# The rows of x loaded ahead of the modulation weights, and their preparation moved into the first unit's slots

## The chip, the cores and the metric

One core of a Trainium2 chip runs the whole program. A core has five engines with an instruction queue each: TensorE (PE, matrix multiplies), VectorE (DVE), ScalarE (ACT), GpSimd (POOL) and SyncE (SP), which here issues every transfer. Engines meet only through semaphores. The metric is the device time of one execution in microseconds (us); lower is better. TensorE's clock has two levels, 2.4 and 1.2 GHz; the profile gives the granted share.

## What is computed

A trunk of two layers over x (1024 rows of 1024, float32). Only the beginning of layer 0 is touched:

```python
shift, scale, gate = ada_modulation(c, a_ada_w[l], a_ada_b[l], 3)   # silu(c) @ w + b
u = rms_norm(h, a_norm_g[l]) * (1 + scale) + shift                  # h = x in layer 0
q, k, v, z = jnp.split(u @ a_w_in[l], 4, axis=-1)
q = rms_norm(q.reshape(bsz, seq, 2 * A_HEADS, A_HEAD_DIM), a_q_norm_g[l])
k = rms_norm(k.reshape(bsz, seq, 2 * A_HEADS, A_HEAD_DIM), a_k_norm_g[l])
...
o = diff_causal_attention(q, k, v, lam, slopes_a)
o = rms_norm(o, a_subln_g[l]) * (1.0 - lambda_init)
o = o.reshape(bsz, seq, A_INNER) * jax.nn.silu(z)
h = h + gate * (o @ a_w_out[l])
```

Then a shared key and value are made from h, and layer 1 attends to them in a window of 128 and adds its own output in the same way.

## The kernel before

**Numbers.** Projections are float32 products in three passes: each factor is split into a rounded part (u_hi, w_hi) and its remainder (u_lo, w_lo), and PE adds u_hi w_hi, u_hi w_lo and u_lo w_hi (L469 to L471). ACT writes the rounded parts, DVE or POOL the remainders.

**The prologue**, in this order:
- SP loads parameters, then the eight 1 MB chunks of the modulation weights (ada_w, 128 x 2048 each) into two buffers in turn, e0 and stage. DVE multiplies each by its column of silu(c) and adds it into adabuf (L1268, L1271), and a buffer is loaded again when DVE is done with it. Then SP loads four chunks of w_a into raw.
- PE adds adabuf up over the partitions with 16 matmuls of one column (L669), DVE makes mod (shift, scale) and smod from it (L1275, L1278).
- Then the row tiles. A row tile is 128 rows of x. For each of eight: load into half of e0, squares summed (ACT, L896), variance (DVE, L1286), seed of the root (ACT, L908 and L910), three Newton steps (DVE, L949 to L954), normalise (DVE, L1296), eight transposes of 128 x 128 into ps_t or ps_s (PE, L680), modulate columns 0 to 3 (DVE, L959) and 4 to 7 (ACT, L903) into e1, u_hi (ACT, L914), u_lo (DVE, L1299). Two tiles are under way at a time. PE projects tiles 0 and 1 of the first unit between the last of these. Of w_a's eight chunks ACT (L693) makes w_hi[0] and POOL (L394) w_lo[0] between the tiles.

**The units.** Layer 0's attention has eight units, one per head, each of eight slots, one per row tile. It is a pipeline written out by hand: in slot i of unit u PE does, in this order, the scores of tile i-3 (L488); the projection of tile i-1, chunks 0 to 2; the second part of the scores, if tile i-3 has one (from tile 4 on); the product with v of tile i-4 (L522); chunk 3; the transposes of qn of tile i-2 (L537); chunks 4 to 6; the transposes of the probabilities of tile i-3 (L544), which wait for the combination of the two softmaxes (a_comb, DVE L1074); chunk 7. A chunk is three matmuls of 512 columns. In slots 1 and 2 of the first unit PE projects nothing, since tiles 0 and 1 are done.
DVE per slot: reduce and variance of the heads' norms (L1017, L1027), masked maxima (L1002), Newton steps, qn (L980), later parts, combination (L1074), w_lo of one chunk of the next unit's weights (split_lo, L928), one step of the later modulation sums into adabuf (L1083 or L1085).
ACT per slot: squares and copies of the projection (L714 to L720), seed, exponentials (L740), gate, kT and qT (L769, L770), w_hi of one chunk (L693), the copy of the transposed probabilities to pT (L775).
POOL per slot: a clamp, the copy to va, the gate's product.

## Time and profile before

| | us |
|---|---|
| median of 3 runs | 1268.44 (1267.43 to 1270.52) |
| the profiled execution | 1270.51 |
| its span | 1268.4 |
| PE busy in the span | 1153.8 (91%) |
| DVE busy | 729.6 (58%) |
| ACT busy | 667.3 (53%) |
| POOL busy | 168.3 (13%) |
| smod written | 41.6 |
| first scores of tile 0 (slot 3 of the first unit) | 100.06 |
| first scores of tile 5 (slot 8) | 140.99 |

The span is the time from the first to the last instruction of the profiled execution; the run's time has some 2 us around it. All times in the trace count from the start of the span. A busy PE is not a PE at its peak, since matmuls are pipelined. The PE clock of the table of stretches is 1.00 up to 95 us, although the matmuls at 77 us stand 0.43 us apart and those at 80 us 0.23: for the beginning the distance of the matmuls tells the clock.

### The profile page before, as it was taken

The page shows a single profiled execution, that of the slowest core. Times are in us where ns is not written, and L with a number is a line of the kernel's source. Part 1 is how long each engine was busy: PE and PEld are TensorE (multiplying, and loading weights), DVE is VectorE, ACT ScalarE, POOL GpSimd, SP SyncE. Part 2 cuts the span into 40 slices and gives each one's busy share as a digit, 9 for nine tenths or more (in the row PEclk, how much of TensorE's full clock was granted, in tenths as well). Part 3 has the DMA queues.
Part 4 walks back from the last instruction along what each step waited for, and adds up shares of the span by engine and source line. Part 5 has one row for each costly group of instructions (what it writes and reads, how often), then busy time and mean ns, then how long its engine had stood idle before and what let it go on. Part 6 is the DMA issues. An engine that isn't in the chain of part 4 may idle for free.

```text
span 1268.4 us, 19295 instructions
## 1 busy us (share of the span) xinstructions
PE 1153.8 (91%) x6048; PEld 897.6 (71%) x6048; DVE 729.6 (58%) x2326; ACT 667.3 (53%) x2045; POOL 168.3 (13%) x301
## 2 busy tenths in 40 slices
PE   0468999999999999999987999869999999997998
PEld 0356777777777777777765888758878878785886
DVE  5466677676767677676765354545555555545221
ACT  0465566565655555655653455546666666664110
POOL 1311111110111111010110111031111111110122
PEclk9998999999999999999996999979999999997999
DMA  8423222232222222232223333210111111123342
GB/s 282 140 92 106 81 81 92 69 92 69 92 70 87 74 72 89 69 93 75 85 64 139 96 109 111 67 58 22 49 41 38 42 47 38 43 60 121 116 133 83
DMA packets 51221, 107.41 MB, mean 85 GB/s; under 512 B 5808, under 2 KB 18224, under 8 KB 49968
## 3 DMA queue, kind: packets, MB, share of 16 engines
q1 hardware_dynamic: 51120, 106.18, 26.6%
q8 instruction: 49, 0.80, 0.3%
q14 instruction: 52, 0.43, 0.1%
HBM read 89.38 MB, written 16.78 MB: 84 GB/s over the span
## 4 chain that ended last, share of the span: by engine, by line
PE 84%; DVE 5%; issue 4%; DMA 3%; ACT 2%; POOL 1%; POOLq 0%; SPq 0%; DVEq 0%; ACTq 0%
PE ps_p L469 15%; PE ps_p L471 14%; PE ps_p L470 14%; PE ps_s L488 6%; PE ps_o L522 5%; PE ps_p L619 4%; PE ps_p L621 4%; PE ps_p L620 4%; PE ps_o L588 3%; PE ps_t L544 3%; PE ps_s L572 2%; PE ps_t L604 2%; DMA stage<-ada_w 2%; PE ps_o L643 2%; PE ps_o L537 1%
## 5 line engine op out<-in xcount | busy, mean ns | idle before, releaser
L469 PE MATMUL ps_p<-w_hi,u_hi 128*128 128x512 f32 x768 | 337.3, 439 | 0.0
L471 PE MATMUL ps_p<-w_hi,u_lo 128*128 128x512 f32 x768 | 304.3, 396 | 0.0
L470 PE MATMUL ps_p<-w_lo,u_hi 128*128 128x512 f32 x768 | 302.9, 394 | 0.0
L469 PEld LDWEIGHTS ps_p<-w_hi,u_hi 128*128 128x128 f32 x768 | 146.5, 191 | 64.2 <-ACT gbuf L720 30.1
L471 PEld LDWEIGHTS ps_p<-w_hi,u_lo 128*128 128x128 f32 x768 | 145.5, 190 | 33.1
L470 PEld LDWEIGHTS ps_p<-w_lo,u_hi 128*128 128x128 f32 x768 | 147.3, 192 | 17.8
L740 ACT ACTIVATE e<-e,negm 128x256 f32<-128x256 f32 (+7 forms) x128 | 98.3, 769 | 99.0 <-DVE negm L1002 97.8
L928 DVE TENSOR_TENSOR w_lo<-raw,w_hi 128x512 fp32r<-128x512 f32 x120 | 81.9, 691 | 102.4 <-ACT w_hi L693 102.4
L405 POOL TENSOR_SCALAR gbuf<-gbuf 128x128 f32<-128x128 f32 (+1 forms) x96 | 37.2, 387 | 589.9 <-ACT gbuf L720 589.9
L488 PE MATMUL ps_s<-kT,qT 64*128 64x512 f32 (+3 forms) x384 | 90.2, 547 | 3.7 <-DVE negm L1002 3.1
L522 PEld LDWEIGHTS ps_o<-va,pT 128*128 128x128 f32 x576 | 72.6, 194 | 17.3 <-issue 13.8
L775 ACT ACTIVATE pT<-ps_t 128x512 f32<-128x512 f32 (+2 forms) x96 | 44.7, 491 | 74.6 <-PE ps_t L544 74.1
L693 ACT ACTIVATE w_hi<-raw 128x512 fp32r<-128x512 f32 x128 | 78.9, 628 | 5.6 <-DMA raw<-w_b 5.6
L522 PE MATMUL ps_o<-va,pT 128*128 128x128 f32 x576 | 78.9, 283 | 0.0
L417 POOL TENSOR_TENSOR gbuf<-stage,gbuf 128x128 f32<-128x128 f32 (+1 forms) x96 | 53.3, 555 | 185.6 <-ACT gbuf L733 183.8
L1002 DVE CUSTOM_DVE_ANT_0 e<-ps_s,bias 128x512 f32<-128x512 f32 (+3 forms) x128 | 70.8, 590 | 10.7 <-PE ps_s L488 6.5
L785 ACT ACTIVATE e<-e,negm 128x256 f32<-128x256 f32 (+1 forms) x128 | 61.8, 484 | 19.2 <-DVE negm L1123 19.1
L1172 DVE TENSOR_TENSOR adabuf<-ps_p,e 128x512 f32<-128x512 f32 x32 | 22.1, 690 | 85.2 <-PE ps_p L621 84.8
L426 POOL TENSOR_TENSOR adabuf<-adabuf,stage 128x1024 f32<-128x1024 f32 x16 | 38.2, 2388 | 245.4 <-DVE adabuf L1172 245.4
L813 ACT ACTIVATE pT<-ps_t 128x512 f32<-128x512 f32 (+1 forms) x64 | 33.0, 568 | 59.9 <-PE ps_t L604 59.8
L1074 DVE SCALAR_TENSOR_TENSOR e<-e,rl 128x512 f32<-128x512 f32 (+2 forms) x96 | 61.0, 663 | 2.3
L588 PEld LDWEIGHTS ps_o<-va,pT 128*128 128x128 f32 x480 | 58.2, 191 | 3.0 <-issue 0.3
(166 smaller groups left out, 2058.8 us busy)
## 6 DMA issues: line engine op xcount, KB each, us to landing
adabuf<-ada_w SPq DMA_DIRECT2D x64, 384.0 KB, 3.4
raw<-w_a SPq DMA_DIRECT2D x80, 256.0 KB, 3.5
raw<-w_b SPq DMA_DIRECT2D x48, 256.0 KB, 3.2
e<-ada_w SPq DMA_DIRECT2D x4, 1024.0 KB, 4.8
stage<-ada_w SPq DMA_DIRECT2D x4, 1024.0 KB, 5.0
e<-x SPq DMA_DIRECT2D x8, 512.0 KB, 3.6
oa_scratch<-gbuf SPq DMA_DIRECT2D x64, 64.0 KB, 1.6
e<-oa_scratch SPq DMA_DIRECT2D x8, 512.0 KB, 3.8
```

The costliest lines, as they stand in the source:

```text
L469: pe.matmul(o, u_hi[:, c, t], w_hi[par][:, c, :], start=(c == 0), stop=False)
L470: pe.matmul(o, u_hi[:, c, t], w_lo[par][:, c, :], start=False, stop=False)
L471: mm = pe.matmul(o, u_lo[:, c, t], w_hi[par][:, c, :], start=False, stop=(c == KD - 1))
L488: mm = pe.matmul(ps_s[:, sub * 512:sub * 512 + hi_k - lo_k], qT[d, it % 2, 0:P], kT[d, 0, lo_k:hi_k], start=True, stop=True)
L522: mm = pe.matmul(ps_o[:, i4 % 2, 0:P], pT[:, j * P:(j + 1) * P], va[:, j, :], start=(j == 0), stop=(j == i4))
L588: mm = pe.matmul(ps_o[:, i4 % 2, j * HD:(j + 1) * HD], pT[:, (2 * j + k) * P:(2 * j + k + 1) * P], va[:, i4 - 1 + k, (j // 2) * HD:(j // 2 ...
L693: act.activation(w_hi[par][:, c, :], raw[:, c % RAW, :], ACT.Copy).then_inc(w_hi_done, 1)
L740: act.activation(e, e, ACT.Exp, scale=-1.0, bias=negm[:, it % 2, sub:sub + 1], accum_out=lsum[:, it % 4, sub:sub + 1]).then_inc(S.e, 1)
L785: last = act.activation(e, e, ACT.Exp, scale=-1.0, bias=negm[:, it % 2, j:j + 1], accum_out=lsum[:, it % 4, j:j + 1])
L928: dve.tensor_tensor(w_lo[par][:, c, :], raw[:, c % RAW, :], w_hi[par][:, c, :].bitcast(F32), ALU.subtract).then_inc(w_lo_done, 1)
L1002: dve.tensor_tensor_reduce(e, ps_s[:, sub * 512:sub * 512 + hi_k - lo_k], bias[:, b0 + lo_k:b0 + hi_k], -1.0, negm[:, it % 2, 2 + sub:3 + ...
L1074: dve.scalar_tensor_tensor(out=e0[:, i3 % 2, c0:c1], in0=e1[:, c0:c1], scalar=rl[:, 1, 0:1], in1=e0[:, i3 % 2, c0:c1], op0=ALU.mult, op1=A ...
```

## The change

- **The queue.** SP loads, without a wait: parameters, rows of tile 0, four chunks of w_a, rows of tiles 1 to 7, seven chunks of the modulation weights, the eighth in two halves, and then w_a's chunks 4 to 7 (which wait for raw to be free). Nothing is loaded into the same place twice before smod: the weights (ada0_in, 64 KB per partition) lie over u_hi and u_lo, and x (x_in, 32 KB) over w_hi[1] and w_lo[1], the weights' buffers of the second unit.
- **The sums.** The one-column matmuls go in two halves of eight, the first of which waits for the first half of the last sum.
- **Before smod** the squares, root, normalising and transposes of tile 0 are done; all of w_hi[0] and w_lo[0] are made then too.
- **The row tiles 1 to 7** are prepared in slots 0 to 6 of the first unit, tile i+1 in slot i: PE transposes its columns 0 to 3 behind chunk 2 and 4 to 7 behind chunk 6 (both before the projection in slot 0), ACT modulates its part at the slot's end, DVE its part behind split_lo, and writes u_lo of it at the next slot's head. From tile 4 on both halves go through the same half of ps_t.
- **Roots** are taken for tiles 0, 1, 2 and 3, and 4 to 7 together. DVE normalises tiles 0 to 3, POOL tiles 4 to 7 (4 and 5 in slot 1, 6 in slot 2, 7 in slot 3).
- PE projects tiles 0 and 1 in slots 1 and 2, like all others.

The diff, cut to its core:

```diff
+        u_at = nc.sbuf_base + (-nc.sbuf_base) % 32
...
+        ada0_in = over(u_at, "ada0_in", [P, KD, ADA0])
...
+            w_at = nc.sbuf_base + (-nc.sbuf_base) % 32
...
+        x_in = over(w_at, "x_in", [P, 2, KD, FW])
...
+        def x_transposed(n, half):
+            if n < 4:
+                return (ps_t, ps_s)[n % 2][:, half * FW:(half + 1) * FW]
+            return ps_t[:, FW:2 * FW]
+        u_mod = kT[:, 1, :]
...
-            big = [flat(e0[:, :, :]), flat(stage[:, :, :])]
-            for c in range(KD):
-                at_least(sp, ada0_used, c - 1)
-                sp.dma_start(big[c % 2], ada0_w[c]).then_inc(ada0_loaded[c % 2], 16)
+            def load_x(n):
+                sp.dma_start(x_rows(n), groups(x[n * P:(n + 1) * P, :], FW)).then_inc(n_x[n], 16)
+            load_x(0)
             for c in range(RAW):
                 load_chunk(0, c, w_a[0, :, c, :])
-            sp.wait_ge(ada0_used, KD)
-            for n in range(NT):
-                at_least(sp, n_tr, n - 1)
-                sp.dma_start(e0[:, n % 2, :], x[n * P:(n + 1) * P, :]).then_inc(n_x[n % 2], 16)
-                if n in (1, 2):
-                    for c in (2 * n + 2, 2 * n + 3):
-                        load_chunk(0, c, w_a[0, :, c, :])
-            sp.wait_ge(ada0_mm, 1)
+            for n in range(1, NT):
+                load_x(n)
+            for c in range(KD - 1):
+                sp.dma_start(ada0_in[:, c, :], ada0_w[c]).then_inc(ada0_loaded[c], 16)
+            for k in range(2):
+                t = slice(k * ADA0 // 2, (k + 1) * ADA0 // 2)
+                sp.dma_start(ada0_in[:, KD - 1, t], ada0_w[KD - 1, :, t]).then_inc(ada0_loaded[KD - 1 + k], 16)
+            for c in range(RAW, KD):
+                load_chunk(0, c, w_a[0, :, c, :])
+            sp.wait_ge(ada0_mm, 2)
...
+                    if is_a and u == 0 and 1 <= i < 4:
+                        if i == 1:
+                            pool.wait_ge(n_rs, 4)
+                        for n in ((4, 5), (6,), (7,))[i - 1]:
+                            pool.tensor_scalar(x_rows(n), x_rows(n), xrs[:, n:n + 1], 1.0, ALU.mult,
+                                               ALU.mult).then_inc(n_norm_late, 1)
...
+            def rows_of_x(n, half):
+                pe.wait_ge(*((n_norm, n + 1) if n < 4 else (n_norm_late, n - 3)))
+                if n >= 4:
+                    pe.wait_ge(*((n_umod_a, n) if half == 0 else (n_umod_d, n + 1)))
+                elif n >= 2:
+                    pe.wait_ge(n_umod_d, n - 1)
+                    pe.wait_ge(n_umod_a, n - 1)
+                for d in range(4):
+                    mm = pe.transpose(x_transposed(n, half)[:, d * P:(d + 1) * P], x_in[:, half, n, d * P:(d + 1) * P],
+                                      ident[:, :])
+                mm.then_inc(n_tr, 1)
...
+                    def next_rows(half):
+                        if first and i < NT - 1:
+                            rows_of_x(i + 1, half)
...
+                    if first and i == 0:
+                        next_rows(0)
...
                     part_of_projection(range(4, 7))
+                    if i:
+                        next_rows(1)
...
-            for s in range(NT + 1):
-                if s >= 1:
-                    n = s - 1
-                    dst = (ps_t, ps_s)[n % 2]
-                    pe.wait_ge(n_norm, n + 1)
-                    at_least(pe, n_umod_d, n - 1)
-                    at_least(pe, n_umod_a, n - 1)
-                    for d in range(KD):
-                        mm = pe.transpose(dst[:, d * P:(d + 1) * P], e0[:, n % 2, d * P:(d + 1) * P], ident[:, :])
-                    mm.then_inc(n_tr, 1)
-                if s in (6, 7):
-                    project(a, True, 0, 0, s - 6, s - 6, range(KD))
+            rows_of_x(0, 0)
+            rows_of_x(0, 1)
+            for k in range(2):
+                pe.wait_ge(ada0_used, KD + k)
+                for j in range(k * 8, k * 8 + 8):
+                    mm = pe.matmul(ps_p[:, 0, j:j + 1], adabuf[:, j * P:(j + 1) * P], ones[:, :], start=True, stop=True)
+                mm.then_inc(ada0_mm, 1)
...
+            def x_modulate(n):
+                act.wait_ge(n_tr, 2 * n + 2)
+                at_least(act, u_ready, n)
+                for d in range(4, KD):
+                    last = act.activation(u_mod[:, d * P:(d + 1) * P], x_transposed(n, 1)[:, (d - 4) * P:(d - 3) * P],
+                                          ACT.Identity, scale=smod[:, 0, d:d + 1],
+                                          bias=mod[:, M_A_SHIFT + d:M_A_SHIFT + d + 1])
+                last.then_inc(n_umod_a, 1)
+                act.wait_ge(n_umod_d, n + 1)
+                act.wait_ge(n_umod_a, n + 1)
+                act.activation(u_hi[:, :, n * P:(n + 1) * P], groups(u_mod, P), ACT.Copy).then_inc(n_hi, 1)
...
+                    if isinstance(u, int) and u == 0 and i < NT - 1:
+                        x_modulate(i + 1)
+                        if i < 2:
+                            for n in range(*x_groups[i + 2]):
+                                x_squares(n)
+                            x_seed(i + 2)
...
+            for c in range(RAW):
+                split_hi(0, c, 0)
+            x_squares(0)
+            x_seed(0)
+            for c in range(RAW, KD):
+                split_hi(0, c, 0)
             act.wait_ge(s_mod, 3)
-            act.wait_ge(bias_a, 1)
...
+            x_modulate(0)
+            x_squares(1)
+            x_seed(1)
...
+            def x_normalise(k, n):
+                dve.wait_ge(n_rs, k + 1)
+                dve.tensor_scalar(x_rows(n), x_rows(n), xrs[:, n:n + 1], None, ALU.mult).then_inc(n_norm, 1)
+            def x_modulate(n):
+                dve.wait_ge(n_tr, 2 * n + 1)
+                at_least(dve, u_ready, n)
+                modulate(x_transposed(n, 0), lambda d: u_mod[:, d * P:(d + 1) * P], 0, M_A_SHIFT, n_umod_d)
+            def x_low(n):
+                dve.wait_ge(n_hi, n + 1)
+                dve.tensor_tensor(u_lo[:, :, n * P:(n + 1) * P], groups(u_mod, P),
+                                  u_hi[:, :, n * P:(n + 1) * P].bitcast(F32), ALU.subtract).then_inc(u_ready, 1)
...
+                    if first and i:
+                        x_low(i)
...
+                    if first and i < NT - 1:
+                        x_modulate(i + 1)
+                        if i == 0:
+                            x_roots(2)
+                            x_normalise(2, 2)
+                        elif i == 1:
+                            x_normalise(2, 3)
+                            x_roots(3)
...
+            x_roots(0)
+            x_normalise(0, 0)
+            acc = adabuf[:, 0:ADA0]
+            for c in range(KD + 1):
+                t, j = slice(0, ADA0), min(c, KD - 1)
+                if c >= KD - 1:
+                    t = slice((c - KD + 1) * ADA0 // 2, (c - KD + 2) * ADA0 // 2)
+                dve.wait_ge(ada0_loaded[c], 16)
...
+            x_modulate(0)
+            x_low(0)
+            x_roots(1)
+            x_normalise(1, 1)
```

How the order of instructions changes. SP, the beginning of its queue, before (ada_w into e and stage: the modulation weights; w_a into raw: the projection's weights):

```order
L352 DMA prm<-par 128x115
L353 DMA gbuf<-rows_in 128x384
L357 DMA e<-ada_w 128x2048
L357 DMA stage<-ada_w 128x2048
...
L293 DMA raw<-w_a 128x512 x4
L363 DMA e<-x 128x1024 x2
```

SP, the same place in the changed kernel:

```order
L385 DMA prm<-par 128x115
L386 DMA gbuf<-rows_in 128x384
L389 DMA x_in_50<-x 128x2x512
L326 DMA raw<-w_a 128x512 x4
L389 DMA x_in_50<-x 128x2x512 x7
L397 DMA ada0_in_49<-ada0_w 128x2048 x7
L400 DMA ada0_in_49<-ada0_w 128x1024 x2
L326 DMA raw<-w_a 128x512 x4
```

All of x and half of w_a have moved ahead of the modulation weights. DVE, first unit, from the combination of slot 3 to the first maxima of slot 4, before (e: the exponentials, sq: squares of the projected heads; kT's second half holds the modulated tile in the changed kernel):

```order
L1074 SCALAR_TENSOR_TENSOR e<-e,rl 128x128 [waits a_ratio]
L928 TENSOR_TENSOR w_lo<-raw,w_hi 128x512 [waits w_hi_done]
L1085 SCALAR_TENSOR_TENSOR adabuf<-adabuf,csil 128x768 [waits ada_acc_done,ada_loaded1]
L1017 TENSOR_REDUCE ssum<-sq 128x4 [waits a_var,a_sq]
L1027 TENSOR_SCALAR var<-ssum 128x4 [waits a_ssum,a_rs]
L1002 ISA e,negm<-ps_s,bias 128x256 [waits a_s]
```

DVE, the same place in the changed kernel:

```order
L1178 SCALAR_TENSOR_TENSOR e<-e,rl 128x128 [waits a_ratio]
L1000 TENSOR_TENSOR w_lo<-raw,w_hi 128x512 [waits w_hi_done]
L1058 TENSOR_SCALAR kT<-ps_t,smod,mod 128x128 [waits u_ready,n_tr]
L1058 TENSOR_SCALAR kT<-ps_t,smod,mod 128x128 x3
L1197 SCALAR_TENSOR_TENSOR adabuf<-adabuf,csil 128x768 [waits ada_acc_done,ada_loaded1]
L1053 TENSOR_TENSOR u_lo<-kT,u_hi 128x8x128 [waits n_hi]
L1121 TENSOR_REDUCE ssum<-sq 128x4 [waits a_var,a_sq]
L1131 TENSOR_SCALAR var<-ssum 128x4 [waits a_ssum,a_rs]
L1101 ISA e,negm<-ps_s,bias 128x256 [waits a_s]
```

Four modulations stand behind w_lo, and u_lo stands ahead of the reduce. PE, first unit, the end of slot 5 in the changed kernel, where before the transposes of e followed at once on the chunk (x_in: the normalised rows; in slots 3 to 6 alike):

```order
L514 MATMUL ps_p<-w_hi,u_lo 128x512
L527 MATMUL ps_t<-ident,x_in 128x128 [waits n_umod_d,n_norm_late]
L527 MATMUL ps_t<-ident,x_in 128x128 x3
L615 MATMUL ps_t<-ident,e 128x128 [waits a_comb]
L615 MATMUL ps_t<-ident,e 128x128 x2
```

A wait for DVE's modulation (n_umod_d) now stands ahead of the one for the combination (a_comb).

## Rows read from the trace of the kernel before

**Rows 1.** Stretches: us, busy (instructions) of PE, PEld, DVE, ACT, POOL; clock, DMA share, GB/s.
```profile
41.62:100.06 58.44, 25.93 (x114) 21.06 (x114) 36.65 (x89) 37.85 (x91) 14.19 (x10) 0.96 0.37 114
100.06:140.99 40.93, 40.93 (x189) 30.30 (x190) 28.73 (x93) 24.45 (x85) 5.78 (x15) 0.93 0.28 90
140.99:1268.40 1127.41, 1080.03 (x5714) 839.35 (x5713) 643.55 (x2119) 603.35 (x1868) 143.56 (x266) 0.97 0.25 77
```

**Rows 2.** Timeline, modulation sums: start us, us, engine, line, operation [idle before].
```profile
9.57 2.35 DVE L1271 SCALAR_TENSOR_TENSOR adabuf<-stage,csil,adabuf 128x2048 f32<-128x2048 f32 x1 [1.10 <-DMA stage<-ada_w]
...
34.14 6.96 PE L669 MATMUL ps_p<-ones,adabuf 128*128 128x1 f32 x32 [34.14 <-DVE oss L1273]
...
41.42 0.17 DVE L1278 SCALAR_TENSOR_TENSOR smod<-mod,prm 128x8 f32<-128x8 f32 x1
```

**Rows 3.** Stretches, the transfers alone: us, then clock, DMA share, GB/s.
```profile
0.00:8.00 8.00, 1.00 0.75 262
4.00:8.00 4.00, 1.00 1.01 414
29.00:34.00 5.00, 1.00 0.93 359
```

**Rows 4.** Timeline, steps of row tiles 0, 1 and 7 in the prologue.
```profile
41.62 1.06 ACT L896 ACTIVATE stage<-e 128x1024 f32<-128x1024 f32 x1 [35.24 <-DVE smod L1278]
...
42.91 0.15 DVE L1286 TENSOR_SCALAR var<-ssum 128x1 f32<-128x1 f32 x1 [1.31 <-ACT stage L896]
...
50.54 0.75 DVE L1296 TENSOR_SCALAR e<-e,rs 128x1024 f32<-128x1024 f32 x1
...
51.35 1.97 PE L680 MATMUL ps_s<-ident,e 128*128 128x128 f32 x8 [3.37 <-DVE e L1296]
...
90.56 1.51 ACT L903 ACTIVATE e<-ps_s,mod,smod 128x128 f32<-128x128 f32 x4 [3.55 <-PE ps_s L680]
...
93.24 1.23 DVE L1299 TENSOR_TENSOR u_lo<-e,u_hi 128x1024 fp32r<-128x1024 f32 x1 [1.32 <-ACT u_hi L914]
```

**Rows 5.** Timeline, DVE's normalising of tile 0 beside POOL's first two remainders.
```profile
44.13 2.95 POOL L394 TENSOR_TENSOR w_lo<-raw,w_hi 128x512 fp32r<-128x512 f32 x2 [38.29 <-ACT w_hi L693]
44.15 1.81 DVE L1296 TENSOR_SCALAR e<-e,rs 128x1024 f32<-128x1024 f32 x1
```

**Rows 6.** PE's restart at slot 2: stretch, timeline, and the chain of waits (start, us).
```profile
95.00:96.00 1.00, 0.00 (x0) 0.80 0.04 6
...
98.75 0.69 PE L537 MATMUL ps_o<-ident,qn 128*128 128x128 f32 x2 [8.23 <-DVE qn L980]
...
105.43 0.43 PE ps_p L470
...
106.35 0.23 PE ps_p L469
```

**Rows 7.** Timeline, slot 4 of the first unit, PE and then DVE.
```profile
109.16 0.70 PE L488 MATMUL ps_s<-kT,qT 64*128 64x256 f32 x4
...
112.90 0.38 PE L537 MATMUL ps_o<-ident,qn 128*128 128x128 f32 x2
...
115.19 0.38 PE L544 MATMUL ps_t<-ident,e 128*128 128x128 f32 x2
...
116.20 0.92 PE L488 MATMUL ps_s<-kT,qT 64*128 64x384 f32 x4
...
109.69 0.42 DVE L1017 TENSOR_REDUCE ssum<-sq 128x4 f32<-128x256 f32 x1 [0.58 <-ACT sq L714]
...
111.69 0.42 DVE L980 TENSOR_TENSOR qn<-ps_p,rs 128x256 f32<-128x256 f32 x1
...
114.40 0.69 DVE L928 TENSOR_TENSOR w_lo<-raw,w_hi 128x512 fp32r<-128x512 f32 x1 [1.44 <-ACT w_hi L693]
```

**Rows 8.** Timeline, slot 7: the first scores, and DVE's second masked maximum.
```profile
131.91 1.13 PE L488 MATMUL ps_s<-kT,qT 64*128 64x512 f32 x4
...
133.84 0.69 DVE L1002 CUSTOM_DVE_ANT_0 e<-ps_s,bias 128x512 f32<-128x512 f32 x1
```

More of the change, by code:

```diff
@@ L155, in build @@
         junk = sb("junk", [P, P])
+        xss = sb("xss", [P, NT])
+        xvar = sb("xvar", [P, NT])
+        xy0 = sb("xy0", [P, NT])
+        xysq = sb("xysq", [P, NT])
+        xrs = sb("xrs", [P, NT])
         def ps(name, shape):
@@ L171, in build @@
         s_lam = sem("s_lam")
-        ada0_loaded = [sem(f"ada0_loaded{k}") for k in range(2)]
+        ada0_loaded = [sem(f"ada0_loaded{k}") for k in range(KD + 1)]
         ada0_used = sem("ada0_used")
@@ L185, in build @@
         bias_step = sem("bias_step")
-        n_x = [sem(f"n_x{k}") for k in range(2)]
+        n_x = [sem(f"n_x{n}") for n in range(NT)]
         n_ss = sem("n_ss")
@@ L1012, in slot @@
                     stats = not (first and i < 2)
+                    if first and i:
+                        x_low(i)
+                    if first and i == 3:
+                        dve.wait_ge(bias_a, 1)
                     if live(2):
```

109 lines of the change are left out of this document (45 added, 64 removed).

## The prediction, written before the changed kernel ran

> **What bounds the kernel now.** I read the table of stretches first [rows 1]. From 140.99 us on TensorE (PE) is busy for 1080.0 of 1127.4 us, and the change leaves that part alone, so all it can win or lose lies before 140.99. There the limits change. Up to 41.6 us loads and VectorE's (DVE) sums over the modulation weights bind, then a 6.96 us block of one-column matmuls [rows 2]. From 41.6 to 100.06 PE works 25.9 of 58.4 us: the eight row tiles of x go one after another through ACT (ScalarE), DVE and PE. From 100.06 to 140.99, slots 3 to 7 of the first unit, PE is never idle. The change takes x's preparation out of the second stretch and puts half of it into the third. So I count to three marks: T0 (smod is written), the first scores of tile 0 (100.06 now), and the end of slot 7 (140.99 now).
>
> **To T0.** In the queue there now stand ahead of the last whole weight chunk: 0.25 MB of parameters, 0.52 of x, 1.05 of w_a, 3.67 of x, and 7.34 of weights, 12.8 MB in all. By 8.0 us the trace moved 262 GB/s x 8 = 2.1 MB, and while two large loads were outstanding (4 to 8 us), 414 GB/s [rows 3]. The rest needs 10.7/0.414 = 25.9 us, so that chunk is there at 33.9. A DVE sum of 2.35 us is shorter than the 2.5 us between chunks, so DVE keeps up. Behind it: its sum 2.35, half a sum 1.2, all 16 one-column matmuls 6.96 (the second half's data comes while the first is multiplied), and 0.5 to smod [rows 2]. T0 = 45.0; it was 41.6. Overlapped loads win, but the 5.2 MB put ahead cost more: +3.4 us. Before, those loads were free later.
> The Trainium skill, "DMA: Bandwidth & Descriptors", section "Bandwidth", says that for loads from HBM the HBM side (about 358 GB/s) binds and not the 435 of the fabric. By 358 the sum would have T0 at 49.0. The 414 of this trace speaks against it, though only over 4 us.
>
> **T0 to the scores of tile 0.** Times from T0; a hand-over is read from rows, not only the work.
> Row 0: from the modulation's start to u_lo's 2.7, u_lo 1.2: 3.9. Then DVE takes row 1's root (1.24 from the variance to the normalising) and the 0.8 us to PE: 5.9. Eight transposes on the slow clock 2.0: 7.9 [rows 4, 5]. ACT: modulation and u_hi 2.6, squares of rows 2 and 3 at 1.1 each, root 1.3, normalising 0.8: PE gets row 2 at 14.9. Meanwhile it has run nine matmuls of tile 0.
> Slot 1: half a row 0.45, twelve matmuls at 0.23, half a row 0.45: 18.6. ACT: 2.6, squares of rows 4 to 7 4.4, root 1.3: 26.9. DVE stands behind that root, since it is ahead in its order of the step on adabuf (1.0) and of u_lo of row 2 (1.2): 29.1.
> Here POOL begins to normalise rows 4, 5 and 6. The trace shows what a POOL operation can do to DVE: when POOL had just begun its two differences, DVE's normalising took 1.81 us [rows 5], and 0.75 without POOL [rows 4], so each meeting costs 1.06. Those were operations with two inputs, these have one, whose meeting no row here shows as clearly; I take the same. DVE meets POOL at its step and at u_lo: +2.1, range 0 to 3.2 (three meetings). The heads' chain for tile 0 (reduce to qn) is 2.2, so PE's transposes of qn start at 33.3. PE has then idled since 22.4.
> Before, PE stopped at 90.5, the granted clock fell in 95 to 96 us, and after the restart matmuls stood 0.43 apart until 105.9 and 0.23 after it [rows 6]. So this stretch is slow again: 0.5, nine matmuls 3.85, half a row 1.0, ACT's modulation of row 3 1.5, for which the scores now wait: 40.1. Before it was 58.4. This is the gain: 18.3 us.
>
> **Slots 3 to 7.** Each of slots 3 to 6 takes on a row (4 to 7). On PE that is 8 transposes, some 0.11 each at full clock (half of [rows 4]): 0.9 per slot. But they close a loop through three engines, which the order shows: ACT modulates behind its copy to pT, DVE writes u_lo at the next slot's head, ahead of the heads' reduce; DVE modulates behind w_lo, and PE can't transpose the second half before that.
> Slot 4 [rows 7]. Its start is the scores (109.16). The reduce began 0.5 after it and qn was written 2.4 later; PE wanted qn 3.7 after the start. Now the reduce begins behind u_lo, 3.6 after the start (below), and PE wants qn at 4.2 but has it at 6.0: a wait of 1.8. From the transposes of qn to the end of w_lo it is 2.2 (112.90 to 114.40 + 0.7), then DVE's modulation 1.4: PE's second half starts at 9.6, where it could at 8.3. With 0.45 and the 1.01 of the slot's rest the next slot starts at 11.1. ACT behind that half: copy to pT done 1.2 after its start, modulation 1.5, u_hi 1.1, u_lo 1.2, in all 5.0, which is 3.6 behind the next start. The loop closes: 11.1 in place of 7.0, +4.0.
> Slots 5 and 6 have longer maxima on DVE and more scores on PE; I take +3.8 each. Slot 3 has a shorter way in (2.3, as the scores already waited for ACT) and comes to 9.5; before it was 9.1, 2.6 of that the slow clock: +0.4. Slot 7 takes no row, but the second part of its scores waits until DVE's first maxima are done, which were 2.6 behind the start and are now 5.7; PE wants them at 3.2 [rows 8]: +2.4. Sum 14.4: 40.9 + 14.4 = 55.3.
>
> **Sum.** 45.0 + 40.1 + 55.3 = 140.4 against 140.99: -0.6 us. The profiled execution has a span of 1268.4 (run time 1270.5), so its span becomes 1267.8; against the median of 1268.44 I say **1267.8 us**. The gain of 18.3 is spent on 3.4 of later weights and 14.4 in the loop. I allow 5 us either way for hand-overs read wrong.
>
> **Rivals.**
> *The loop doesn't bind (faster).* If ACT and DVE reach the rows early enough, slots 3 to 7 cost only PE's 3.5 us of transposes less the 2.6 of slow clock: 41.8 in place of 55.3, 1254.3. For it: DVE is busy 28.7 and ACT 24.5 of 40.9 us there [rows 1]. Against: it is the order that waits, not the load. Chance 0.12.
> *The clock stays low in slots 3 to 6 (slower).* With PE waiting twice a slot, matmuls at 0.43. A slot has 7.7 us of PE work at full clock, 14.4 at half: 3.3 more than 11.1, times four, with 2.9 in slots 1 and 2: +16, 1284. It decides when waits of 1 to 2 us are enough; in the trace it fell only behind 5.3 us of nothing [rows 6]. Chance 0.08.
> *The loads don't hold 414 GB/s.* From 29 to 34 us, with five loads of two kinds outstanding, it was 359 at a share of 0.93 [rows 3]. At that rate 10.7 MB take 29.8: T0 +3.9, 1271.7. Chance 0.12. It is also what the Trainium skill's section named above would give.
> *Slow clock in slot 1 too.* The nine matmuls aren't enough to raise it, and row 2 is 2.9 later: 1270.7. Chance 0.12.
>
> **Chances.** The forecast case has 0.56 and runs from 1262.5 to 1272.5. A measurement of this kernel can tell 0.3%, 3.8 us: below 1264.6 or above 1272.2. Faster: 0.12 and 0.14 of the forecast case, 0.26. Slower: 0.08, 0.06 of the forecast case and 0.04 of each of the last two, 0.22. Same: 0.52. For 8 in 10 the range goes from 1260 to 1275; the two outer rivals stay outside.
>
> **What would show it.** Right: smod near 45 us; the first scores of tile 0 near 85; in slots 3 to 6 starts 11 us apart with PE waiting for qn and for DVE's modulation, one to two us each; slot 7's end near 140. Each mark can fail alone: T0 by the rate, the second by ACT's squares and POOL's meetings with DVE, the third by the loop. Wrong in kind: slots 3 to 6 at 8 us without waits, matmuls 0.43 apart in slot 4, or a change behind slot 7.

## The result, and the profile after

The changed kernel took **1277.35 us** (median of 4 runs, 1276.61 to 1281.11) against 1268.15 for the kernel before: ratio 1.0069, 95% interval 1.0055 to 1.0083. A second set gave 1277.77 against 1270.32, ratio 1.0062 (1.0047 to 1.0077). So the change costs 7.5 to 9 us. I had said 1267.8 with a range up to 1275; the measured time lies above it.

The stretches of the changed kernel, cut as in [rows 1] (columns as there), but that the last mark stands 0.22 us ahead of the first scores of slot 8, which start at 151.45:
```profile
51.94:95.03 43.09, 21.65 (x75) 16.98 (x75) 19.69 (x45) 21.51 (x51) 6.89 (x6) 0.76 0.22 69
95.03:151.23 56.20, 43.46 (x221) 30.98 (x221) 37.53 (x112) 33.75 (x104) 6.23 (x15) 1.00 0.18 57
151.23:1279.30 1128.07, 1080.40 (x5715) 840.11 (x5713) 643.53 (x2119) 603.71 (x1869) 143.57 (x266) 0.98 0.25 77
```
smod is written at 51.94 (41.6 before), the scores of tile 0 come 43.1 us behind it (58.4 before), slots 3 to 7, up to 151.45, take 56.4 us (40.93 before), and all behind them is nearly what it was: 1127.85 us against 1127.41. That part of the forecast stands: the change was decided in the first 151 us.

The first stretch, answering [rows 2] and [rows 3]. First the transfers, then the timeline of DVE and PE:
```profile
0.00:8.00 8.00, 0.00 (x0) 0.00 (x0) 2.81 (x15) 2.17 (x4) 4.77 (x10) 1.00 0.67 193
4.00:8.00 4.00, 0.00 (x0) 0.00 (x0) 2.71 (x13) 0.68 (x2) 1.70 (x2) 1.00 0.94 307
8.00:40.00 32.00, 0.00 (x0) 0.00 (x0) 16.59 (x12) 3.49 (x8) 4.98 (x4) 1.00 1.02 407
```
```profile
22.89 1.28 DVE L1385 TENSOR_SCALAR adabuf<-ada_in,csil 128x2048 f32<-128x2048 f32 x1 [8.19 <-DMA ada_in<-ada_w]
25.38 12.30 DVE L1388 SCALAR_TENSOR_TENSOR adabuf<-ada_in,csil,adabuf 128x2048 f32<-128x2048 f32 x5 [1.20 <-DMA ada_in<-ada_w]
37.83 4.93 DVE L1388 SCALAR_TENSOR_TENSOR adabuf<-ada_in,csil,adabuf 128x2048 f32<-128x2048 f32 x3
42.71 0.06 DVE L1390 MEMSET oss<- 128x1 f32 x1
42.89 1.94 PE L527 MATMUL ps_t<-ident,x_in 128*128 128x128 f32 x8 [42.89 <-DVE oss L1390]
44.62 6.82 PE L743 MATMUL ps_p<-ones,adabuf 128*128 128x1 f32 x32
...
51.77 0.17 DVE L1395 SCALAR_TENSOR_TENSOR smod<-mod,prm 128x8 f32<-128x8 f32 x1
```
Two things are to be seen. DVE stands idle for 8.2 us before its first sum, and from the second on its sums follow each other without a gap at 2.46 us each: once chunks come, they come fast enough, but the first comes late. And PE transposes tile 0 only at 42.89, released by `oss`, a memset that has nothing to do with x, although the first tile of x had been normalised since about 14.7 us.

The second stretch (answers [rows 4] and [rows 6]; PE and ACT, then DVE and POOL):
```profile
57.84 1.97 PE L527 MATMUL ps_s<-ident,x_in 128*128 128x128 f32 x8 [6.40 <-DVE x_in L1044]
...
66.89 1.12 PE L527 MATMUL ps_t<-ident,x_in 128*128 128x128 f32 x4 [3.76 <-DVE x_in L1044]
...
73.42 1.50 ACT L813 ACTIVATE kT<-ps_t,mod,smod 128x128 f32<-128x128 f32 x4 [7.44 <-PE ps_t L527]
...
88.07 0.69 PE L606 MATMUL ps_o<-ident,qn 128*128 128x128 f32 x2 [10.80 <-DVE qn L1079]
...
95.03 0.49 PE L544 MATMUL ps_s<-kT,qT 64*128 64x128 f32 x4 [0.98 <-ACT kT L813]
...
84.10 0.41 DVE L1121 TENSOR_REDUCE ssum<-sq 128x4 f32<-128x256 f32 x1
84.54 0.57 DVE L1131 TENSOR_SCALAR var<-ssum 128x4 f32<-128x4 f32 x1
...
86.23 1.06 DVE L1023 SCALAR_TENSOR_TENSOR yh<-ysq,var 128x5 f32<-128x5 f32 x1
...
82.21 5.08 POOL L443 TENSOR_SCALAR x_in<-x_in,xrs 128x1024 f32<-128x1024 f32 x3 [34.63 <-DVE xrs L1039]
```
And the slots (answers [rows 7] and [rows 8]): the scores that start slots 4 to 7, the late second part of slot 7, and then what PE waited for from 95 us to 151 (us in total, times, longest; the waits at L606 are those of the transposes of qn, L1155 is DVE's scaling of an earlier tile's output, which reads the same buffer):
```profile
104.61 0.70 PE L544 MATMUL ps_s<-kT,qT 64*128 64x256 f32 x4
...
115.66 0.92 PE L544 MATMUL ps_s<-kT,qT 64*128 64x384 f32 x4
...
127.43 1.13 PE L544 MATMUL ps_s<-kT,qT 64*128 64x512 f32 x4
...
139.69 1.13 PE L544 MATMUL ps_s<-kT,qT 64*128 64x512 f32 x4
...
145.42 0.49 PE L544 MATMUL ps_s<-kT,qT 64*128 64x128 f32 x4 [2.32 <-DVE negm L1101]
...
151.45 1.13 PE L544 MATMUL ps_s<-kT,qT 64*128 64x512 f32 x4
...
PE ps_t L527 <- DVE kT L1058: 4.7, 4, 1.2
PE ps_o L606 <- DVE gbuf L1155: 3.5, 2, 1.8
PE ps_s L544 <- DVE negm L1101: 2.3, 1, 2.3
PE ps_o L606 <- DVE qn L1079: 2.2, 2, 1.6
```
The slots are 9.6, 11.1, 11.8, 12.3 and 11.8 us long. In each of the four that take a row PE waits 1.2 us for DVE's modulation, and 0.6 to 1.8 us ahead of the transposes of qn: the loop of the forecast.

### The profile page after: what moved, and what is told of

Same layout as the page of the kernel before. It is cut to its first block, busy times and chain, and to the rows that moved or that the text cites. A ratio compares the mean times of both kernels' runs of the same rounds, so it can differ in the third digit from the quotient of the medians.

```text
span 1279.3 us, 19274 instructions
## 1 busy us (share of the span) xinstructions
PE 1154.1 (90%) x6048; PEld 896.6 (70%) x6048; DVE 723.2 (57%) x2307; ACT 667.1 (52%) x2037; POOL 172.3 (13%) x305
## 4 chain that ended last, share of the span: by engine, by line
PE 80%; DVE 6%; issue 5%; ACT 4%; DMA 3%; SPq 1%; POOL 1%; POOLq 0%; DVEq 0%; ACTq 0%
PE ps_p L512 14%; PE ps_p L514 13%; PE ps_p L513 13%; PE ps_s L544 6%; PE ps_o L591 5%; PE ps_p L690 4%; PE ps_p L692 4%; PE ps_p L691 4%; PE ps_o L659 3%; PE ps_t L615 3%; PE ps_s L643 2%; PE ps_t L675 2%; DMA ada_in<-ada_w 2%; PE ps_o L714 2%; PE ps_o L606 1%
## 5 line engine op out<-in xcount | busy, mean ns | idle before, releaser
L861 ACT ACTIVATE pT<-ps_t 128x512 f32<-128x512 f32 (+2 forms) x96 | 44.7, 491 | 81.9 <-PE ps_t L615 81.5
```

## The experiments

Each run's median is set against the kernel before on the same chip: 1268.2 for the changed kernel, 1268.8 for e1 to e4, 1267.8 for e5, e9, e10 and e11, 1270.3 for its second set, e6, e13 and e14. So kernels of different groups are compared by their ratios, which have 95% intervals of 0.0011 to 0.0023 either way (1.4 to 2.9 us). From each profile I take three marks: smod written, the first scores of tile 0, and the start of slot 7.

| kernel | smod | first scores | between | slots 3 to 6 | median, us | ratio to before |
|---|---|---|---|---|---|---|
| before | 41.6 | 100.1 | 58.4 | 31.9 | 1268 to 1270 | |
| changed | 51.9 | 95.0 | 43.1 | 44.7 | 1277.4 | 1.0069 |
| changed, again | 50.8 | 92.6 | 41.8 | 44.7 | 1277.8 | 1.0062 |
| e1 constant first | 47.9 | 91.1 | 43.3 | 44.7 | 1276.7 | 1.0062 |
| e2 weights first | 42.4 | 83.8 | 41.4 | 44.7 | 1270.1 | 1.0012 |
| e3 low part later | 50.8 | 91.5 | 40.7 | 44.2 | 1275.2 | 1.0057 |
| e5 pieces of 4 KB | 49.5 | 92.8 | 43.3 | 44.7 | 1277.9 | 1.0078 |
| e10 gap filled | 50.9 | 91.3 | 40.4 | 44.7 | 1276.4 | 1.0062 |
| e4 prepared early | 51.9 | 75.4 | 23.5 | 44.7 | 1260.4 | 0.9935 |
| e9 late rows on DVE | 48.6 | 73.5 | 24.9 | 44.7 | 1258.4 | 0.9924 |
| e11 weights first, prepared | 50.4 | 75.3 | 24.8 | 44.7 | 1258.7 | 0.9924 |
| e13 late rows in slot 1 | 38.7 | 73.3 | 34.6 | 44.7 | 1257.4 | 0.9905 |
| e14 e13 and e3 | 38.7 | 71.1 | 32.4 | 44.2 | 1256.9 | 0.9897 |
| e6 e4 and loop order | 51.5 | 72.7 | 21.2 | 42.0 | 1254.7 | 0.9878 |

### What the order of the queue costs (e2, e5, a1)

```diff
-            for n in range(1, NT):
-                load_x(n)
...
             sp.wait_ge(ada0_mm, 2)
```
e2 moves these two lines behind the chunks of modulation weights and changes nothing else.

> Against the changed kernel, only the place of the loads of tiles 1 to 7 of x in the queue: behind the modulation weights, ahead of chunks 4 to 7 of w_a. My theory: 3.67 MB leave the way of the weights, at the 0.40 MB/us of this stretch 9.1 us; smod comes at 42.8 and everything behind it 9 us earlier (about 1268.3), since tile 1 is asked for only 2.6 us behind smod and has landed by 35. Rival: the beginning of the queue is slow whatever stands there (307 GB/s from 4 to 8 us), and the weights take that over: 7 us. Rival: ACT's squares of tiles 2 to 7 wait for loads or PE for w_lo of chunks 4 to 7, and half of it is lost again: 4 to 5 us.

1270.14 us, ratio 1.0012 (1.0001 to 1.0023). By the ratios the queue order alone is worth 6.3 to 7.2 us, nearly all of the loss; with it undone the rebuilt beginning is within 3 us of the kernel before. smod came as the theory had it (42.4), the time as its first rival. In its timeline PE's transposes, again released by the memset, and the first scores:
```profile
32.66 1.94 PE L527 MATMUL ps_t<-ident,x_in 128*128 128x128 f32 x8 [32.66 <-DVE oss L1390]
...
83.79 0.49 PE L544 MATMUL ps_s<-kT,qT 64*128 64x128 f32 x4 [0.99 <-ACT kT L813]
```
smod comes 8.4 to 9.5 us sooner than in the two profiles of the changed kernel, and the first scores 8.8 to 11.2. From smod to the scores it is 41.4 us (41.8 in the second profile), so nothing there waits for the rows of x. Of this gain 1.3 us are lost again in slot 7: behind PE's wait of 2.32 us there the clock is granted at 0.50 from 135.8 to 139.2, and the slot takes 13.0 us in place of 11.8.

The changed kernel again, and then with x in pieces twice as long:

> The changed kernel once more, for a second trace of its beginning beside the versions of this call. Theory, the first profiled execution was 1.1 us late in its loads (its first chunk of modulation weights landed at 22.9 where the versions with the same queue order had it at 21.7 to 21.9): here the first sum starts at 21.7 to 22, smod is written at 50.7 to 51, 43.1 us before the first scores of tile 0, and VectorE's memset of the scalar that TensorE waits for still stands behind the last sum; the time is 1277 again. Rival, the loads of that execution were the usual ones: smod at 51.9 again.

> The changed kernel, with the rows of x laid in SBUF as one piece of 4 KB per partition and row tile where it has two of 2 KB; nothing else changes. Theory, the first 8 us of loading are slow (307 GB/s from 4 to 8 us where the kernel before had 414) because x comes in pieces of 2 KB: they go at 380 GB/s or more, the last whole chunk of modulation weights lands near 35 us where it landed at 37.8, smod is written near 49 (51.9), and the time falls by 2 to 3 us against the changed kernel, to about 1275. Rival, the slow start is one of the queue (the first transfers of a program, whatever they carry): the rate from 4 to 8 us stays near 307 GB/s, smod stays at 51 to 52, the time is that of the changed kernel, 1277.

```diff
-        x_in = over(w_at, "x_in", [P, 2, KD, FW])
+        x_in = over(w_at, "x_in", [P, 2, 4, D])
...
-            return x_in[:, :, n, :]
+            return x_in[:, n % 2, n // 2, :]
...
-                sp.dma_start(x_rows(n), groups(x[n * P:(n + 1) * P, :], FW)).then_inc(n_x[n], 16)
+                sp.dma_start(x_rows(n), x[n * P:(n + 1) * P, :]).then_inc(n_x[n], 16)
```
The transfers from 4 to 8 us, in the second profile of the changed kernel and then in e5, and the first sum of each:
```profile
4.00:8.00 4.00, 0.00 (x0) 0.00 (x0) 2.66 (x13) 0.69 (x2) 1.70 (x2) 1.00 0.96 318
...
21.80 1.28 DVE L1385 TENSOR_SCALAR adabuf<-ada_in,csil 128x2048 f32<-128x2048 f32 x1 [7.45 <-DMA ada_in<-ada_w]
```
```profile
4.00:8.00 4.00, 0.00 (x0) 0.00 (x0) 2.16 (x13) 1.31 (x4) 1.97 (x3) 1.00 1.02 373
...
20.50 1.28 DVE L1385 TENSOR_SCALAR adabuf<-ada_in,csil 128x2048 f32<-128x2048 f32 x1 [6.56 <-DMA ada_in<-ada_w]
```
The first profile was indeed 1.1 us late in its loads (22.89); four other profiles with this queue order (a1, e1, e3, e10) have the first sum at 21.7 to 21.9. But a1's scores stand 41.8 us behind smod and not the 43.1 expected. With 4 KB pieces the rate from 4 to 8 us is 373 GB/s, just under the 380 of the theory, the first sum starts 1.3 us sooner and smod is written at 49.5, 1.3 us under a1. The time did not fall (1277.86), against the theory. In the profiles the gain is gone at the scores: from smod to them it is 43.3 us in e5 and 41.8 in a1. That is the clock, below.

### The wait on a constant (e1)

```diff
+            dve.memset(oss[:, :], 0.0).then_inc(s_const, 1)
             x_roots(0)
             x_normalise(0, 0)
...
-            dve.memset(oss[:, :], 0.0).then_inc(s_const, 1)
             dve.wait_ge(ada0_mm, 2)
```


> Against the changed kernel, with one line moved: DVE's memset of oss, which gives the fourth count of s_const, stands ahead of the modulation sums. My theory: PE's first instruction waits for s_const >= 4, so the transposes of tile 0 (1.94 us) and the first half of the one-column matmuls could only begin at 42.9, behind the last sum; now the transposes are done at 17, the first half begins at 41.5, smod comes at 48.9 in place of 51.9, and the kernel takes 3 us less (about 1274.3). Rival: PE would have waited for the sums anyway and only the transposes lay in the way: 1.4 to 1.9 us less. Rival: no change, since the last half sum binds.

```profile
14.67 1.94 PE L527 MATMUL ps_t<-ident,x_in 128*128 128x128 f32 x8 [14.67 <-DVE x_in L1044]
...
40.38 6.99 PE L743 MATMUL ps_p<-ones,adabuf 128*128 128x1 f32 x32 [23.77 <-DVE adabuf L1389]
```
PE transposes tile 0 28 us sooner, and the block of one-column matmuls starts beside the last half sum instead of behind transposes that stand behind all sums. smod is written at 47.9, 3.0 us sooner than in a1, whose first sum started at the same time. The median fell by 0.6 to 1.0 us and not by the 3 of the theory; the runs can't tell that from nothing. Again the profile shows half of it lost before the scores: 43.3 us from smod to them, 1.5 more than in a1.

### The clock in slot 1 (e10)

```diff
+                    if first and i == 1:
+                        for _ in range(14):
+                            pe.transpose(ps_o[:, 1, 0:P], ident[:, :], ident[:, :])
                     if i:
                         next_rows(0)
```


> The changed kernel, with 14 more transposes of the identity (into a buffer that nobody reads) on TensorE in slot 1, between the first part of tile 0's projection and the transposes of row tile 2, where it stood idle for 3.8 us; they leave nothing out and no one waits for them. Theory, it was that gap after which the clock fell to 0.50 for some 6 us: with the gap filled the granted clock stays at full level through slot 1, VectorE's modulation of row 2 comes 2.9 us sooner after smod, and so do the first scores of tile 0 (40.2 us after smod where it was 43.1); the time falls by 2 to 3 us, to about 1274.5. Rival, the clock falls there whatever TensorE does (it follows the whole beginning): the first scores stay 43 us after smod and the time stays at 1277.

The stretch from 66 to 70 us, where PE takes row 2 and goes on with tile 0: the changed kernel, the same again, and e10 (the last three numbers are clock, DMA share, GB/s).
```profile
66.00:70.00 4.00, 3.12 (x10) 2.63 (x11) 3.96 (x9) 0.00 (x0) 0.00 (x0) 0.50 0.40 124
```
```profile
66.00:70.00 4.00, 4.00 (x14) 3.22 (x13) 3.92 (x8) 0.00 (x0) 0.00 (x0) 0.57 0.46 164
```
```profile
65.86 0.66 PE L527 MATMUL ps_t<-ident,x_in 128*128 128x128 f32 x4 [1.94 <-DVE x_in L1047]
...
66.00:70.00 4.00, 4.00 (x22) 3.38 (x22) 4.00 (x8) 0.24 (x1) 0.00 (x0) 1.00 0.53 166
```
With the junk in the gap, PE's idle time ahead of row 2 shrinks to 1.9 us (3.8 in the first profile, 4.5 in the second) and the granted clock stays at 1.00. The twelve matmuls of 512 columns between the two halves of row 2 take 2.9 us, where they took 5.1 and 4.4. The scores stand 40.4 us behind smod: 2.7 less than in the first profile, 1.4 less than in the second. So the theory holds in this one trace. In the time it isn't shown: 1276.40 us is 1.0 to 1.4 less than the changed kernel, but the ratio is 1.0062 (1.0041 to 1.0083), that of its second set.

The stretch at 0.50 in slot 1 is 6.8 us long in the first profile (65.8 to 72.6), e1 and e5, with the scores 43.1 to 43.3 us behind smod, and 3.4 us long in a1 (66.5 to 69.9), e2 and e3, with the scores 41.8, 41.4 and 40.7 behind it. So in the profiles of e1 and e5 the longer one took back 1.5 us of the gain over a1. Whether it also explains their medians isn't shown, since each kernel has one profiled execution.

### Preparing x before smod (e4, e9, e11)

e4 takes the constant early and moves the squares, the roots, the normalising and the transposes of tiles 0 and 1 ahead of smod, where ACT and POOL stood idle and DVE waited 8 us for its first chunk. In the code of DVE (ACT, POOL and PE likewise):
```diff
+            for k, tiles in enumerate(((0,), (1,), (2, 3), ())):
+                x_roots(k)
+                for n in tiles:
+                    x_normalise(k, n)
```


> Against the changed kernel, with the line of e1 and: ACT's squares and the roots of all eight tiles, DVE's normalising of tiles 1 to 3, POOL's of 4 to 7 and PE's transposes of tile 1 are done before smod, while the weights still load (ACT is idle from 13.6 to 41 us there). My theory: between smod and the first scores of tile 0 squares, roots and normalising stood on the path (43.1 us in the changed kernel); without them that stretch is bound by the modulation of tile 0, two projections half on the slow clock and the heads' chain, some 22 us. smod at 48.9 as in e1, first scores at 71, the slots as before: 24 us less than the changed kernel, 1253. Rival: the slow clock and the hand-overs of the modulated tiles bind that stretch, and only squares and POOL's share go: 10 us less beside e1's 3. Rival: POOL's four operations beside DVE's sums delay smod by 4 us or more, and half of the gain is lost.

1260.36 us, ratio 0.9935 (0.9915 to 0.9954): 16.4 us under e1 on the same chip, but 7 above the theory's 1253. The scores stand 23.5 us behind smod in place of 43.1. smod itself comes at 51.9, although e1 had it at 47.9, so the last rival came true with its 4 us; and in slot 7 the clock is low from 127.1 to 130.5, which costs 1.3 us as in e2. DVE and POOL in its timeline, and then DVE in e9, which takes POOL's pieces away:
```profile
24.86 21.68 DVE L1377 SCALAR_TENSOR_TENSOR adabuf<-ada_in,csil,adabuf 128x2048 f32<-128x2048 f32 x8
...
23.64 11.44 POOL L432 TENSOR_SCALAR x_in<-x_in,xrs 128x1024 f32<-128x1024 f32 x4 [10.82 <-DVE xrs L1031]
```
```diff
-                    for n in range(4, NT):
-                        pool.tensor_scalar(x_rows(n), x_rows(n), xrs[:, n:n + 1], 1.0, ALU.mult,
-                                           ALU.mult).then_inc(n_norm_late, 1)
...
+            for n in range(4, NT):
+                dve.tensor_scalar(x_rows(n), x_rows(n), xrs[:, n:n + 1], None, ALU.mult).then_inc(n_norm_late, 1)
             dve.wait_ge(ada0_mm, 2)
```


> The kernel with the preparation of x ahead of smod, with the normalising of row tiles 4 to 7 taken from GpSimd and put on VectorE behind the sums, in VectorE's wait for the matmuls of the modulation. Theory, GpSimd's 11.4 us pieces stretched VectorE's sums from 17.4 to 21.7 us: without them the sums take 17.5 to 19 (GpSimd's low parts of the weights are still beside some of them), smod is written 2.5 to 4 us sooner, near 48.5, the first scores of tile 0 still 23.7 us behind it, and the time falls from 1260.4 to 1257 to 1258. Rival, the sums wait for loaded weights and not for GpSimd: smod stays at 51 to 52, and the time at 1260.

```profile
24.30 18.23 DVE L1372 SCALAR_TENSOR_TENSOR adabuf<-ada_in,csil,adabuf 128x2048 f32<-128x2048 f32 x8
```
The sums take 18.2 us in place of 21.7 and smod comes 3.3 us sooner; the first scores 1.9 us sooner (73.5). The time is 1258.41, by the ratios 1.4 us less, within their intervals. These are the forecast's meetings of POOL and DVE at another place: POOL's four pieces cost the sums 3.5 us. The Trainium skill, "SBUF — State Buffer", section "Who interferes with whom", says that a DVE instruction with two inputs in SBUF contends with a GpSimd instruction that reads SBUF. The sums have two such inputs, and the runs agree: 2.71 us each on average in e4 and 2.28 in e9 (of the eight in a row, two are halves). POOL's pieces suffer as well: 2.86 us each there, where the one at 88.75 us of the changed kernel took 1.12.

> The rows of x behind the modulation weights in the queue again, and their squares, roots and normalising done by ScalarE and VectorE between the sums and smod, in the time of the matmuls of the modulation; all row tiles are normalised on VectorE. Theory, neither load has to be first: the sums run from 15.3 to 32.6, the rows are prepared by about 41, smod is written near 43 (41.5 in the kernel before), the first scores of tile 0 stand 23 to 24 us behind it, near 67, where they stood at 100 in the kernel before and 95.0 in the changed one, and the slots behind keep 9.6 to 12 us; the time is 1248 to 1252. Rival, the preparation delays smod or the loop gives the gain back: smod at 47 or later and a time at 1255 or above.

Here the weights are loaded first, and x is prepared between the sums and smod. The rival won: smod at 50.4, 1258.65 us (expected 1248 to 1252). DVE and POOL:
```profile
43.26 6.28 POOL L430 TENSOR_TENSOR w_lo<-raw,w_hi 128x512 fp32r<-128x512 f32 x4 [29.48 <-ACT w_hi L747]
43.28 6.79 DVE L1380 TENSOR_SCALAR x_in<-x_in,xrs 128x1024 f32<-128x1024 f32 x4
```
DVE got the squares of rows 4 to 7 from ACT only at 42, and then its four normalisings took 1.70 us each beside POOL's remainders; without POOL one takes 0.75 (a row of e6, 12.88 us, and of a1, 64.96, read 0.75).

### Two tries at both (e13, e14), and the loop (e3, e6)

```diff
+                        if i == 1:
+                            x_roots(3)
+                            dve.wait_ge(n_rs, 4)
+                            for n in range(4, NT):
+                                dve.tensor_scalar(x_rows(n), x_rows(n), xrs[:, n:n + 1], None,
+                                                  ALU.mult).then_inc(n_norm_late, 1)
```


> The rows of x behind the modulation weights, prepared in the time of the matmuls of the modulation as before, but with roots and normalising of row tiles 4 to 7 moved to slot 1, into VectorE's wait for row 2. Theory, in the run before VectorE waited until 43.3 for the squares of these rows and then took 6.8 us for them beside GpSimd's low parts: without them VectorE writes smod as soon as the matmuls of the modulation are done, near 43 (50.3), the first scores of tile 0 stand 24 to 25 us behind it, near 67.5 (75.3), and the time falls from 1258.7 to 1250 to 1252. Rival, the 3 us of normalising in slot 1 land on the path of the heads of tile 0 and GpSimd's work slows VectorE there: the first scores at 70 or later, 1254.

1257.35 us, ratio 0.9905 (0.9886 to 0.9925), above the theory and the rival (1254). The rival's first scores came (73.3), but for a cause neither had. smod is written at 38.7, sooner than in any other kernel, and nobody can use it:
```profile
38.56 0.17 DVE L1391 SCALAR_TENSOR_TENSOR smod<-mod,prm 128x8 f32<-128x8 f32 x1
...
45.30 1.97 DVE L1045 TENSOR_TENSOR u_lo<-kT,u_hi 128x1024 fp32r<-128x1024 f32 x1 [5.17 <-ACT u_hi L812]
...
58.69 0.16 DVE L1026 TENSOR_TENSOR xysq<-xy 128x4 f32<-128x4 f32 x1 [5.10 <-ACT xy L800]
```
ACT is still at the squares and at the high parts of the weights until 42.7, so u_hi of tile 0 is late by 4 us; and in slot 1 DVE waits 5.1 us for a root from ACT. The bound had moved to ACT's order; that splitting ACT's squares would give the time back isn't shown. In slot 7 the clock is low from 123.4 to 130.2, and the slot takes 14.5 us in place of 11.8.

```diff
-                    if first and i:
-                        x_low(i)
...
                     if live(2):
                         head_norm(S, s, i2)
+                    if first and i:
+                        x_low(i)
```


> Against the changed kernel, only DVE's u_lo of the tile in slots 1 to 7 moved: from the slot's head to behind qn. My theory of a closed loop: qn comes some 1 us earlier in slots 4 to 6, but u_lo's 1.15 us now stands ahead of the combination, w_lo and DVE's modulation, for which PE waits: the wait for qn falls from 1.6 to 0.7 us, the one for the modulation rises from 1.2 to about 1.6; per slot 0 to 0.5 less, slot 7 1.1 less: 1 to 3 us in all. Rival (u_lo ahead of the reduce is the price of the slots, the rest has room): the waits for qn, 0.6 + 1.6 + 1.8 + 1.7, and for the maxima, 2.3, go: 7 to 8 us less.

1275.17 us. That is 2.2 us under the changed kernel, as the theory had it, but by the ratios 0.6 to 1.5, which the runs can't tell from nothing. PE's waits from 91.5 us on in this kernel:
```profile
PE ps_t L527 <- DVE kT L1058: 5.4, 4, 1.6
PE ps_o L606 <- DVE gbuf L1155: 4.3, 3, 2.1
PE ps_s L544 <- DVE negm L1101: 1.5, 1, 1.5
...
PE ps_t L615 <- DVE e L1178: 0.7, 1, 0.7
PE ps_o L606 <- DVE qn L1079: 0.7, 1, 0.7
```
Taking u_lo out of the way of the heads removes 1.5 us of waits for qn and 0.8 for the maxima. It adds 0.8 at the same transposes (for L1155), 0.7 at the modulation and 0.7 at the combination: nearly all that no longer waits for one step waits for the next. Slots 3 and 4 are 0.5 us shorter each, 5, 6 and 7 0.3 longer each, in all 56.3 us for 56.4. So the profile shows no gain in the slots from this edit alone. The same edit on e13:

> The kernel e13 with VectorE's low part of each row behind the normalising of the heads in slots 1 to 7. Theory, the 2.2 us that this gave in the changed kernel come here too: 1248 to 1250. Rival, in slot 1 and 2 the row's low part is now what TensorE waits for, since the beginning is shorter: no gain over e13, or up to 2 us lost.

1256.87 us against 1257.35, not to be told apart by the runs, so the rival came and not the theory's 1248 to 1250. In the profile the scores come 2.2 us sooner and slots 3 to 6 take 0.45 less.

e6 puts on e4 both this and the modulation ahead of the splitting of a weight chunk:
```diff
-                    split_for(u, i, par, live, units, U_A)
                     if first and i < NT - 1:
                         x_modulate(i + 1)
+                    split_for(u, i, par, live, units, U_A)
```


> The kernel with the preparation of x ahead of smod (1260.4), and in the slots of the first unit VectorE's low part of row i behind the normalising of the heads (as in the run that gained 2.2) and VectorE's modulation of row i+1 ahead of its splitting of a weight chunk. Theory, each slot waits in turn for the heads and for VectorE's modulation (1.2 us a slot): both waits shrink, the slots take 9 to 11.5 us where they took 9.6 to 12.3, and the time falls by 3 to 6 us to 1254 to 1257. Rival, the loop's period is set by the chain through the modulation alone: only the 2 us of the low parts come, 1258.

```profile
114.63 1.13 PE L542 MATMUL ps_s<-kT,qT 64*128 64x512 f32 x4
...
PE ps_t L525 <- DVE kT L1050: 1.8, 2, 1.0
```
**1254.72 us, ratio 0.9878** (0.9864 to 0.9893), the lowest median of the study: 5.6 us under e4, by the ratios 7.2, about what the theory gave. Slots 3 to 6 take 42.0 us in place of 44.7, and PE's waits for the modulation fall from 4.7 to 1.8 us. As e3's edit alone gave hardly anything there, it should be the modulation's new place, alone or together with that edit, that shortens the loop; it wasn't run alone. The scores come 21.2 us behind smod. Slot 5 takes 12.3 us, more than the theory's 11.5 and than in e4 (11.8): the clock is granted at 0.50 there from 99.3 to 102.7, behind a wait of 2.06 us. It isn't combined with e9.

Behind slot 7 the profiles differ too: 1127.4 to 1128.0 us in the changed kernel, e1, e3, e5 and e10, and 1124.4 to 1126.2 in the seven kernels under 1271 us. No run here says why, so 1 to 4 us of each of their gains aren't accounted for by the marks.

## Why the prediction was wrong, point by point

The profiled execution has a span of 1279.3 where I had 1267.8: 11.5 us. The four terms account for it: 6.9 to smod, 3.0 from there to the scores, 1.1 in the slots, 0.4 behind them. The other executions are 3.4 to 4.5 us shorter than the profiled one; the profile of a1 (1276.4) splits its 8.6 into 5.8, 1.7, 1.1 and nothing. The step that failed is T0: its load term was too small, and a wait was left out of it. The clock in slot 1 came on top.

**To T0: mis-sized by 6.9 us, for two reasons.**
*The load, +3.9.* I had chunk 6 at 33.9; its sum starts at 37.8. Six intervals of 2.53 us further up, chunk 0 was to land at 18.7, and it landed at 22.9 (21.8 in the usual executions), so all of the error lies before the first chunk. I had used 2.1 MB by 8 us and 414 GB/s behind it. The trace has 193 GB/s x 8 = 1.5 MB by 8 us, and 407 GB/s behind it. The 414 was nearly right. The 2.1 MB was a number of a kernel that loads large chunks at first; the changed kernel loads x and w_a first, and with 2 KB pieces that goes at 307 to 318 GB/s where the other had 414. That is 0.5 MB, 1.3 us. The rest is that transfers overlap: by 21.8 us of a1 some 7.2 MB had been moved (1.6 by 8 us, 8 us at 393 GB/s, 5.8 at 415), and only 6.5 stand ahead of the end of chunk 0. The 0.6 MB between them are 1.5 us. Here an arrival isn't the sum of the bytes ahead of it over the rate, but that plus what has been begun of the next ones. My rival put the error in the sustained rate, by the Trainium skill's "DMA: Bandwidth & Descriptors", section "Bandwidth". It had almost the right price (+3.9) with the wrong cause: the trace holds 407 GB/s over 32 us. The Trainium skill, "HBM Reference", section "Specifications (TRN2)", says that a core streaming alone measures well above the 358 (about 425); this trace agrees with 407, and I had read only the first figure.
*The wait on `s_const`, +3.1.* I let the one-column matmuls start 1.2 us before the end of the last sum. PE had to transpose tile 0 first, and those transposes wait for the count that the memset behind the sums gives (42.89). The wait was in the order of the instructions that I had before me, as one of three that stand at the first transposes; I read the others, and took this one for a constant of the first microseconds. It even stands in a row that I showed: in [rows 2] the one-column matmuls of the kernel before are released by `oss`, where they came behind the last sum in any case and the wait cost nothing. e1 shows its price in the changed kernel: 3.0 us at smod.

**T0 to the scores: 43.1 for 40.1.** The hand-overs were right: row 1 reaches PE 5.9 us behind T0 (5.9), row 2 at 14.95 (14.9). Then ACT modulates row 2 at 21.5 and not at 18.6, and that 2.9 stays until the end. It is the rival "slow clock in slot 1", which I had at 0.12 and 2.9 us. I took full clock since PE had just run nine matmuls; but it then stood for 3.8 us, and the clock was granted at 0.50. In e10, with the gap cut to 1.9 us, it was not. Behind that the small terms stand, each beside its forecast: ACT's four squares with modulation and root 8.5 us (8.3), the chain from the reduce to the transposes of qn 3.97 beside POOL where it is 2.2 alone, so POOL costs 1.8 (2.1, though I had placed it at two other operations of DVE), and from these transposes to the scores 6.96 (6.85).

**Slots 3 to 7: 56.4 for 55.3.** The loop is there and has its size: 9.6, 11.1, 11.8, 12.3, 11.8 for 9.5, 11.1, 11.4, 11.9, 11.5. The waits are those named. Slots 5 and 6 are each 0.4 longer than I took, because I gave them the surcharge of slot 4 less 0.2, where each needed 0.2 more; slot 7's 0.3 lie behind its second scores. In nine kernels with this order slots 3 to 6 take 44.65 to 44.68 us, whatever happened before them: the loop's length is set by its own order. The clock stayed at 1.00 there, against the second rival. But the rival's condition is no empty one: waits of 2.1 to 2.3 us were followed by the low clock in slot 5 of e6 and in slot 7 of e2, e4 and e13, where the same 2.3 us in the changed kernel were not. That the trace of the kernel before had the fall only behind 5.3 us of nothing was no argument against it.

**The sum.** I had a gain of 18.3 us spent on 3.4 and 14.4. Measured, a gain of 15.4 (58.4 to 43.1) is spent on 10.3 at smod and 15.5 in the slots. The sign of each part was right; the miss came mostly from the smallest part, which I took for the safest.

**What stays open.** Whether the slower start of the x loads is all a matter of the length of the pieces (e5 got 373 of the 414), why the dip of the clock in slot 1 is now 3.4 and now 6.8 us long, and what shortens the part behind slot 7 in the faster kernels.

## What to carry to other kernels

When work is moved ahead in time, go through every wait of its first instruction, not only those on its own data: a constant written far down another engine's program holds it just as well, and costs most where the work was meant to be early. And ask who has to be early: here loading x first delayed the sums that all else waited for by 8 to 9 us, while preparing x first, in time that ACT and DVE had to spare, was worth 16 (e4 against e1).

A gain of a few microseconds ahead of a pipeline that starts and stops need not arrive at its end. Look for what stands behind it: a gap after which the clock falls, the order of the next engine (e13), or a loop whose period the gain doesn't touch.
